# Low parts of three half groups per gate/up chunk: from VectorE to accumulating transfers, with ScalarE taking two of them one pair earlier

## The reference, cut to what matters

```
def swiglu_ffn(x, norm_g, w_gate, w_up, w_down):
    h = rms_norm(x, norm_g)
    return (jax.nn.silu(h @ w_gate) * (h @ w_up)) @ w_down      # 2048 -> 5632 -> 2048
```

## Time and profile before

| what | value |
|---|---|
| median of 3 runs | 2097.47 us |
| the profiled execution, its own time | 2096.73 us |
| its span in the trace | 2094.6 us |
| granted TensorE clock | 1.00 |
| TensorE matmul busy | 2076.8 us, 99% of the span |
| VectorE busy | 1731.5 us, 83% |
| ScalarE busy | 1150.4 us, 55% |
| GpSimd busy | 41.9 us, 2% |
| DMA, hardware queue | 398.50 MB, 55.1% of the 16 engines' time |

### The profile page before, as it was taken

The page is one execution under the profiler, slowest core; times in us unless marked ns, Lnnn a source line. Parts: engine busy times, 40 slices in busy tenths (PEclk is TensorE's granted clock), DMA queues, the critical chain, the costliest instruction groups (busy, mean ns, idle before and its releaser), DMA issues.

```text
span 2094.6 us, 24421 instructions
## 1 busy us (share of the span) xinstructions
PE 2076.8 (99%) x9394; PEld 1709.2 (82%) x9394; DVE 1731.5 (83%) x1907; ACT 1150.4 (55%) x1392; POOL 41.9 (2%) x47
## 2 busy tenths in 40 slices
PE   9999999999999999999999999999999999999999
PEld 8888888888888888888888888878888888888887
DVE  5466579999899998998566666589999899988997
ACT  6444555555455554556666655465555455554553
POOL 1000000000000000000011001000000000000000
PEclk9999999999999999999999999999999999999999
DMA  8655545656465664555554454545556464665554
GB/s 327 207 174 177 181 155 208 220 187 215 160 223 181 215 209 173 207 181 202 198 184 162 159 181 166 173 154 203 209 199 205 171 224 166 221 216 175 193 191 151
DMA packets 203614, 403.19 MB, mean 192 GB/s; under 512 B 8080, under 2 KB 8688, under 8 KB 203248
## 3 DMA queue, kind: packets, MB, share of 16 engines
q1 hardware_dynamic: 202720, 398.50, 55.1%
q0 software_dynamic: 784, 3.19, 0.4%
HBM read 399.56 MB, written 2.10 MB: 192 GB/s over the span
## 4 chain that ended last, share of the span: by engine, by line
PE 63%; DVE 33%; issue 3%; ACT 1%; DMA 0%; SPq 0%; DVEq 0%; ACTq 0%
PE acc L1468 10%; PE acc L1472 10%; PE acc L1470 10%; PE acc L1609 9%; PE acc L1610 9%; PE acc L1611 9%; DVE w_lo L1160 6%; DVE s_lo L1165 5%; DVE sums_b L1149 4%; DVE s_lo L1168 3%; DVE sums_b L1152 2%; DVE sums_b L1155 2%; DVE s_lo L1171 2%; DVE sums_b L1191 1%; DVE stage L1187 1%
## 5 line engine op out<-in xcount | busy, mean ns | idle before, releaser
L741 ACT ACTIVATE w_hi<-raw 128x1024 fp32r<-128x1024 f32 x320 | 326.5, 1051 | 165.4 <-PE acc L1611 151.0
L1160 DVE TENSOR_TENSOR w_lo<-raw,w_hi 128x1024 fp32r<-128x1024 f32 x320 | 380.8, 1217 | 21.2 <-ACT w_hi L741 21.2
L730 ACT ACTIVATE s_hi<-sums_b 128x1024 fp32r<-128x1024 f32 x208 | 209.4, 1053 | 236.5 <-DVE sums_b L1155 235.6
L1609 PE MATMUL acc<-w_hi,a_hi 128*128 128x512 f32 x736 | 288.1, 391 | 1.3 <-DVE w_lo L1160 1.3
L1611 PE MATMUL acc<-w_hi,a_lo 128*128 128x512 f32 x736 | 286.6, 389 | 0.0
L1610 PE MATMUL acc<-w_lo,a_hi 128*128 128x512 f32 x736 | 286.4, 389 | 0.0
L1468 PE MATMUL acc<-w_hi,a_hi 128*128 128x512 f32 x640 | 254.6, 398 | 0.4 <-DVE a_lo L987 0.4
L961 DVE TENSOR_TENSOR w_lo<-raw,w_hi 128x1024 fp32r<-128x1024 f32 x127 | 154.8, 1236 | 116.7 <-ACT w_hi L579 116.6
L1472 PE MATMUL acc<-w_hi,a_lo 128*128 128x512 f32 x640 | 249.6, 390 | 0.0
L1470 PE MATMUL acc<-w_lo,a_hi 128*128 128x512 f32 x640 | 249.2, 389 | 0.0
L730 ACT ACTIVATE s_hi<-raw 128x1536 fp32r<-128x1536 f32 x104 | 154.6, 1486 | 114.1 <-PE acc L1611 114.1
(11 more groups left out here) (223 smaller groups left out, 3793.8 us busy)
## 6 DMA issues: line engine op xcount, KB each, us to landing
raw<-in_ffn_w_down_dram SPq DMA_DIRECT2D x68, 1024.0 KB, 5.0
raw<-in_ffn_w_gate_dram SPq DMA_DIRECT2D x46, 1024.0 KB, 5.8
raw<-in_ffn_w_up_dram SPq DMA_DIRECT2D x46, 1024.0 KB, 5.0
raw<-in_ffn_w_gate_dram SPq DMA_DIRECT2D x84, 512.0 KB, 3.8
raw<-in_ffn_w_up_dram SPq DMA_DIRECT2D x84, 512.0 KB, 5.1
raw<-in_a_w_in_dram SPq DMA_DIRECT2D x30, 1024.0 KB, 5.3
raw<-in_ffn_w_down_dram SPq DMA_DIRECT2D x40, 512.0 KB, 4.8
raw<-in_a_w_out_dram SPq DMA_DIRECT2D x16, 1024.0 KB, 4.9
```

The costliest lines, as they stand in the source:

```text
L730: nc.scalar.activation(s_hi[:, operands, :], src, ACT.Copy).then_inc(s_cast, 1)
L741: ins = nc.scalar.activation(w_hi[:, m % RING, :, :], src, ACT.Copy)
L1160: nc.vector.tensor_tensor(w_lo[:, m % RING, :, :], raw[:, slot, half * HG:(half + 1) * HG, :], w_hi[:, m % RING, :, :].bitcast(F32), ALU.s ...
L1609: nc.tensor.matmul(bank[:, :], hi, rhs_hi, start=start, stop=False)
```

## The change

Three half groups of every block of kind "chunk" go through the `ADDED` path: g7, u4 and u5. In ScalarE's order u4 moves from behind s1 to ahead of it, and u5 from behind s2 to ahead of it. Nothing else changes; the other kinds of block stay as they are.

```
-    ADDED = {"chunk": [], "first": [], "down 0": [], "down 1": [], "down middle": []}
+    ADDED = {"chunk": items("g7 u4 u5"), "first": [], "down 0": [], "down 1": [], "down middle": []}
-    ACT_ORDERS = {"chunk": items("g4 g5 g6 g7 s0 s1 u4 s2 u5 s3 u6 u7")}
+    ACT_ORDERS = {"chunk": items("g4 g5 g6 g7 s0 u4 s1 u5 s2 s3 u6 u7")}
```

## The result

The changed kernel takes 2074.95 us (median of 4 runs, 2074.55 to 2075.15) against 2097.44 us of the kernel before in the same session: 22.5 us less, a ratio of 0.9892 with a 95% interval of 0.988 to 0.9904. The forecast was 2077.3 us in a range of 2074.5 to 2096.0. The span of the profiled execution fell from 2094.6 to 2072.8 us, by 21.8 us.

A forecast was written before the change was run, and what follows sets the result against it. TensorE was taken to set the time, waiting in chunks for VectorE's subtractions. Removing 20.2 us of these waits, with casts and transfers hidden, from the 2097.47 us median gave 2077.3 us, range 2074.5 to 2096.

The forecast's parts named there:

- Where TensorE waited: In chunks, TensorE waits for VectorE's first subtraction of a pair (`s_lo`), mostly before s1; these waits should vanish.
- The balance of 7.66 against 7.49 us a pair: In chunks, VectorE needs 7.66 us for a pair with a half group, TensorE 7.49: VectorE 0.17 us too slow.
- 20.2 us for what TensorE lost: TensorE's loss to late `s_lo` in 18 of 20 chunks, mostly 1.01 to 1.10 us each; all 20.2 us should go.
- A chunk of 41.8 us: Expected duration of one chunk in the changed profile, in place of 42.88 us.
- ScalarE's casts are covered: Three more casts a chunk, 3.1 us, stay hidden; s1's first cast starts 0.25 us late with 1.2 us of cover.
- The transfers' cover: Time from second cast to TensorE's wish: g7 11.5 us, u4 9.7, u5 10.5; no stall expected.
- signs that I had given for being wrong: Transfers over 9.7 us, TensorE waiting for a DMA at L1609, or `s_lo` waits staying although VectorE has gaps.
- rival A: Transfers too slow: at 13.8 us TensorE waits 4.1 us a chunk ahead of u4, 2159 us; decides from 10.7 us; chance 0.11.
- 8.2 us for the transfer: Assumed duration of each 512 KB adding transfer on GpSimd's queue, taken from a 1 MB transfer, between 3.8 and 13.8 us.
- B (VectorE holds up GpSimd): VectorE's subtractions delay GpSimd's descriptor making up to 7.5 us, TensorE late by 6.0 us a chunk: 2197 us; chance 0.03.
- C (a part given back): Cover before s1 or of u5's casts is smaller, or single transfers late: 8 us given back, 2085 us; chance 0.16.
- D (no change): Transfers land near 10.7 us, so TensorE waits at u4 instead of s1: 2093 to 2101 us; chance 0.08.

The follow-up runs named there:

- the long delay: Against the changed kernel, GpSimd does fifteen small memsets in turn ahead of each adding transfer's issue: 2094.95 us, ratio 0.9987 to the kernel before.

## Why the prediction was right, step by step

**Where TensorE waited.** Right. The waits for `s_lo` are gone from the trace, and putting VectorE's time back (2096.27 us) puts them back. The balance of 7.66 against 7.49 us a pair is borne out by g7 alone: one subtraction of 1.13 us less suffices for 20.8 us.

**20.2 us for what TensorE lost.** Right in kind and 1.6 us short in the profiled executions (21.8). Both have the same 9394 matmuls in the same order, so their starts can be set against each other one by one. In the feed-forward parts the long steps (over 0.26 us) are 20.6 us shorter, about what I had counted. The steps of 0.23 to 0.24 us that followed each wait are plain again, which is 1.7 us more and which I had left out of the sum. The one late transfer costs 0.4. Together that is 21.9 us, 10.7 in layer 0 and 11.2 in layer 1. What the sum had too small is the loss behind a wait: I counted 0.11 us on the next step alone.

**A chunk of 41.8 us.** 41.69 to 41.73. This is the same miss: the period was to fall by 1.09 and fell by 1.17.

**ScalarE's casts are covered.** Right. The 0.25 us that I charged to s1's first cast did not come about: VectorE does the sums of s0 0.6 us earlier, so `hidden_hi` starts at 381.29 where it was 381.87, u4's casts end at 384.24 and not at 384.9, and TensorE is itself 0.35 us later in this chunk (389.94 against 389.59). So 0.77 us of cover is left in front of s1.

**The transfers' cover.** The order of 9.7, 10.5 and 11.5 us was right, and two of the sizes were low. From the end of u4's second cast to TensorE's wish it is 394.93 - 384.24 = 10.7 us, for u5 402.41 - 391.00 = 11.4; g7's is the 11.5 that I gave. The one wait for a transfer in the whole run is at u4 in the first chunk after "first":

```profile
352.56 0.39 PE L1611 MATMUL tr<-s_hi,f_lo 128*128 128x512 f32 x1
353.10 0.50 PE L1609 MATMUL acc<-w_hi,a_hi 128*128 128x512 f32 x1
```

0.31 us over a step, and 0.11 for the weights, behind a transfer issued at 342.4 that took 10.7 us. So two of the signs that I had given for being wrong did appear, a transfer over 9.7 us and a wait for a DMA at L1609, at one transfer of 60 and for 0.42 us. All others landed in time. The tightest cover was undersized by 1.0 us, and the decision point of rival A with it; with a true cover of 9.7 us three more of u4's transfers, which took 9.4 us and more, would have been on the edge or over it.

**8.2 us for the transfer.** That the median is just this number is luck, and the argument behind it held only in part. I had taken it from a 1 MB load. Alone the transfer takes 4.4 us, about as long as the 512 KB load of 3.8; it is only beside 1 to 2 MB of loads that it takes 6.9 to 10.7. For g7 the lower bound was nearly the truth, for u4 and u5 the middle. The Trainium skill (DMA: Bandwidth & Descriptors, Anatomy of one DMA, SWDGE path) gives 2.0 us plus the bytes at 436 GB/s, by which I had estimated 4.4 us for 1 MB read; g7's 4.4 us agrees, and with loads alongside the page's sum no longer holds.

**The rivals.** A (too slow) did not happen, but it is real: with ScalarE's order of before it costs 149 us over the changed kernel, and with 3.5 us of delay 20 of the 22.5 us are lost again. B (VectorE holds up GpSimd) is out: 60 issues took 0.836 to 0.941 us beside a VectorE that is busy 39.4 of 41.7 us. That agrees with the Trainium skill (SBUF — State Buffer, Who interferes with whom), by which two-input VectorE instructions contend with GpSimd's reads of SBUF and not with its writes. C (a part given back) has one wait of 0.42 us to show. D (no change) is out by the ratio's interval.

The two halves of the change do different things. The lists in `ADDED` win the time, the order in `ACT_ORDERS` only makes it safe to win it with u4 and u5. That u4 and u5 add 1.3 us to what g7 alone wins (2076.24 to 2074.95) is within what a measurement here can tell from nothing, 4.2 us. The starts in the feed-forward parts of the two traces give 1.3 us as well: 1.7 us less behind VectorE, less the 0.42 of the late transfer.

## What to carry to other kernels

Where two engines are in near balance, a wait of one on the other is worth the excess of the slower one and little more: count it from the starts of the bound engine, and expect that the first piece of relief takes nearly all of it. A long transfer that takes the place of a short instruction needs its operands issued a whole unit of work earlier; give each one a time of wish and a time of issue, and look at which loads run in between, since that doubled its duration here (4.4 to 8.7 us). When a wait of some microseconds is put in front of TensorE, the lost time includes what its clock does afterwards (2.3 us behind waits of 5.4, in the mean).

## What the runs showed of the hardware that I had not expected

- Behind each of the 20 waits of the old order (4.8 to 6.3 us by the starts) TensorE made 6 to 14 steps at about half the pace, 0.43 us in place of 0.227 and the first 0.59. With the long delay the waits of 4.0 and 2.9 us by the starts did the same, with 12 and 7 such steps, and the others, of 1.5 us at most, did not. The longer of the two:

```profile
356.96 0.80 PE L1612 MATMUL acc<-w_hi,a_hi 128*128 128x512 f32 x1 [3.83 <-DMA w_lo<-raw]
357.55 0.63 PE L1613 MATMUL acc<-w_lo,a_hi 128*128 128x512 f32 x1
```

- An adding transfer of 512 KB from tile to tile takes 4.3 to 4.5 us when no load is under way, where a plain load of the same size takes 3.8 in the median, and its issue takes GpSimd 0.85 us. All 60 of them raised the share of GpSimd's queue by 7.7% of 16 engines over 2072.8 us, 160 us for 31.5 MB or 2.7 us of all engines each, a rate of some 197 GB/s of added data.
- A wait costs TensorE more than its length: 0.11 us on the next step, and steps of 0.23 to 0.24 us for a few matmuls after that.
